# Sums of a stick-breaking attention: fp32 matmuls in four-byte passes, or a rounded high and low part

## What is computed

```python
z = jnp.einsum('bqhd,bkhd->bhqk', q_blk, kh).astype(jnp.float32) * scale
mask = k_pos[None, :] < q_pos[:, None]
log_keep = jnp.where(mask, jax.nn.log_sigmoid(-z), 0.0)
between = lax.cumsum(log_keep, axis=3, reverse=True) - log_keep
a = jnp.where(mask, jnp.exp(jax.nn.log_sigmoid(z) + between), 0.0)
return jnp.einsum('bhqk,bhkd->bqhd', a.astype(vh.dtype), vh)
```

## Time and profile before

| | us |
|---|---|
| Time before, median of 3 runs | 1922.7 (1922.46 to 1922.76) |
| The profiled execution, its own time | 1923.37 |
| Span of its profile | 1921.6 |
| TensorE busy | 1907.6 (99%) |
| VectorE busy | 1290.8 (67%) |
| ScalarE busy | 1030.5 (54%) |
| GpSimd busy | 188.0 (10%) |
| First stick layer, from the logits of pair 0 to the wait at the end of `second` | 1192 to 1242 |
| Second stick layer, the same | 1660 to 1710 |

### The profile page before, as it was taken

One profiled execution on the slowest core, in us unless ns is written; L12 is line 12 of the kernel. 1 busy time (PEld: TensorE's weight loads), 2 busy tenths in 40 slices (PEclk: granted clock), 3 DMA queues, 4 the chain that ended last, 5 costly groups with the idle time before them and its releaser, 6 DMA issues.

```text
span 1921.6 us, 27900 instructions
## 1 busy us (share of the span) xinstructions
PE 1907.6 (99%) x10702; PEld 1657.5 (86%) x10702; DVE 1290.8 (67%) x1348; ACT 1030.5 (54%) x1193; POOL 188.0 (10%) x163
## 2 busy tenths in 40 slices
PE   9999999999999999999999999999999999999998
PEld 8888889888888887788888889888888888988887
DVE  5866766766776677666676666776667666667665
ACT  5544564544554457654464446754455445665443
POOL 2800122100010001100010001210001000301000
PEclk9999999999999999999999999999999999999999
DMA  8655644555565553555556566366555556645653
GB/s 307 221 188 184 195 154 149 198 179 196 190 204 190 185 162 122 180 192 196 197 181 205 184 193 201 114 208 199 182 194 197 181 190 198 197 132 186 193 183 105
DMA packets 262420, 356.19 MB, mean 185 GB/s; under 512 B 9040, under 2 KB 230736, under 8 KB 262352
## 3 DMA queue, kind: packets, MB, share of 16 engines
q1 hardware_dynamic: 258752, 342.15, 54.6%
q0 software_dynamic: 3600, 13.11, 1.9%
HBM read 354.18 MB, written 1.05 MB: 185 GB/s over the span
## 4 chain that ended last, share of the span: by engine, by line
PE 87%; DVE 1%; ACT 1%; issue 0%; DVEq 0%; POOLq 0%; POOL 0%
PE down L585 26%; PE gate_banks L464 13%; PE up_banks L464 12%; PE gate_banks L469 7%; PE up_banks L469 6%; PE up_banks L527 4%; PE up_banks L448 3%; PE up_banks L449 3%; PE up_banks L450 3%; PE up_banks L533 2%; PE gate_banks L625 1%; PE gate_banks L655 1%; PE up_banks L479 0%; PE up_banks L481 0%; PE up_banks L480 0%
## 5 line engine op out<-in xcount | busy, mean ns | idle before, releaser
L1445 DVE TENSOR_TENSOR w_lo<-raw,w_hi 128x2048 fp32r<-128x2048 f32 x309 | 706.7, 2290 | 285.8 <-ACT w_hi L1028 285.7
L1028 ACT ACTIVATE w_hi<-raw 128x2048 fp32r<-128x2048 f32 x321 | 611.4, 1905 | 211.6 <-PE down L585 176.9
L464 PE MATMUL gate_banks<-h_both,w_hi 128*128 128x512 f32 x1280 | 305.9, 391 | 0.0
L464 PEld LDWEIGHTS gate_banks<-h_both,w_hi 128*128 128x128 f32 x1280 | 235.7, 188 | 46.1
L464 PE MATMUL up_banks<-h_both,w_hi 128*128 128x512 f32 x1152 | 273.7, 390 | 0.0
L585 PE MATMUL down<-w_hi,m_hi 128*128 128x512 f32 x832 | 269.2, 395 | 2.2 <-DVE m_lo L1538 1.0
L585 PE MATMUL down<-w_lo,m_hi 128*128 128x512 f32 x832 | 265.4, 390 | 0.0
L585 PE MATMUL down<-w_hi,m_lo 128*128 128x512 f32 x832 | 265.2, 390 | 0.0
L464 PEld LDWEIGHTS up_banks<-h_both,w_hi 128*128 128x128 f32 x1152 | 215.7, 188 | 44.5
L585 PEld LDWEIGHTS down<-w_hi,m_lo 128*128 128x128 f32 x832 | 156.2, 188 | 33.3
L585 PEld LDWEIGHTS down<-w_lo,m_hi 128*128 128x128 f32 x832 | 156.3, 188 | 33.0
(11 more groups left out here) (245 smaller groups left out, 2155.5 us busy)
## 6 DMA issues: line engine op xcount, KB each, us to landing
raw<-in_ffn_w_gu SPq DMA_DIRECT2D x88, 1024.0 KB, 5.1
raw<-in_ffn_w_down SPq DMA_DIRECT2D x88, 1024.0 KB, 4.9
raw<-in_ffn_w_gate SPq DMA_DIRECT2D x44, 1024.0 KB, 5.3
raw<-in_ffn_w_up SPq DMA_DIRECT2D x44, 1024.0 KB, 5.3
raw<-in_w_in SPq DMA_DIRECT2D x20, 1024.0 KB, 5.4
raw<-in_ret_w_in SPq DMA_DIRECT2D x13, 1024.0 KB, 5.4
raw<-in_w_o SPq DMA_DIRECT2D x8, 1024.0 KB, 5.0
raw<-in_w_out SPq DMA_DIRECT2D x8, 1024.0 KB, 4.9
```

The costliest lines, as they stand in the source:

```text
L464: mm(banks[:, j * 2 * S:(j + 1) * 2 * S], w_hi[:, r, c:c + P], h_both[:, k, :, :].rearrange("p a b -> p (a b)"), start=(k == 0), stop=(k = ...
L1028: act_fn(w_hi[:, r, 0:width], raw[:, r, 0:width], ACT.Copy).then_inc(hi_ready, 1)
L1445: v.tensor_tensor(w_lo[:, r, 0:width], raw[:, r, 0:width], w_hi[:, r, 0:width].bitcast(f32), ALU.subtract).then_inc(lo_ready, 1)
```

## The change

The sums of a pair are no longer done in plain fp32. ScalarE copies `z_lk` to a high part in fp32r (`keep_high`), VectorE subtracts it to get a low part (`keep_low`), and TensorE multiplies both with the triangle (384 columns in one matmul) and with the ones (128 columns), with weights that are an fp32r copy of the two constants (`exact`, made once in each layer). The parts lie in the then unused rows 4 to 7 of `m_hi` and `m_lo`. At the end of the layer `pair_min(3)` stands ahead of `convolve(0)`, and the low part of the pool ahead of `convolve(1)`.

```diff
+        lk_hi = m_hi[:, 4:7, :].rearrange("p a b -> p (a b)").rearrange("p (a b) -> p a b", a=2)
+        lk_lo = m_lo[:, 4:7, :].rearrange("p a b -> p (a b)").rearrange("p (a b) -> p a b", a=2)
+        exact = m_hi[:, 7, :]
...
                     def pair_sums(s):
-                        pe.wait_ge(s_lk, c0 + s + 1)
-                        tri, ones = cst("tri"), cst("ones")
-                        for g in range(2):
-                            lk, z = z_lk[:, g, :], mid[2 * (s % 2) + g]
-                            mm(z[:, 0:S], tri, lk[:, 0:S], start=False, stop=True, skip_group_check=True)
-                            mm(z[:, P:S], ones, lk[:, S:CAUSAL], start=False, stop=True, skip_group_check=True)
-                            last = mm(z[:, S:CAUSAL], tri, lk[:, S:CAUSAL], start=False, stop=True, skip_group_check=True)
+                        for ready, lk in ((s_lk_hi, lk_hi), (s_lk_lo, lk_lo)):
+                            for g in range(2):
+                                pe.wait_ge(ready, 2 * (c0 + s) + g + 1)
+                                mm(mid[2 * (s % 2) + g][:, 0:CAUSAL], exact[:, 0:P], lk[:, g, :], start=False, stop=True, skip_group_check=True)
+                            for g in range(2):
+                                last = mm(mid[2 * (s % 2) + g][:, P:S], exact[:, P:2 * P], lk[:, g, S:CAUSAL], start=False, stop=True, skip_group_check=True)
                         last.then_inc(s_cs, 1)
...
+                        def keep_high(s):
+                            for g in range(2):
+                                sc.wait_ge(s_lk, 2 * (c0 + s) + g + 1)
+                                act_fn(lk_hi[:, g, :], z_lk[:, g, :], ACT.Copy).then_inc(s_lk_hi, 1)
                         pair_log(0)
                         high(b + 7)
+                        keep_high(0)
                         high(b + 8)
                         pair_exp(0)
                         pair_log(1)
                         pair_high(0)
+                        keep_high(1)
                         high(b + 9)
                         pair_exp(1)
                         pair_log(2)
                         high(b + 10)
                         pair_high(1)
+                        keep_high(2)
                         high(b + 11)
                         pair_exp(2)
                         pair_log(3)
                         pair_high(2)
+                        keep_high(3)
                         high(b + 12)
...
+                        ve.wait_ge(const_in, 16)
+                        for i, name in enumerate(("tri", "ones")):
+                            v.tensor_copy(exact[:, i * P:(i + 1) * P], cst(name)).then_inc(exact_ready, 1)
                         slot_out(2)
...
+                        def keep_low(s):
+                            for g in range(2):
+                                ve.wait_ge(s_lk_hi, 2 * (c0 + s) + g + 1)
+                                v.tensor_tensor(lk_lo[:, g, :], z_lk[:, g, :], lk_hi[:, g, :].bitcast(f32), ALU.subtract).then_inc(s_lk_lo, 1)
                         pair_keep(0)
+                        keep_low(0)
                         slot_out(4)
                         low(b + 7)
                         slot_out(5)
                         pair_min(0)
                         low(b + 8)
                         pair_keep(1)
+                        keep_low(1)
                         slot_out(6)
...
+                        pair_min(3)
                         convolve(0)
-                        pair_min(3)
-                        convolve(1)
                         ve.wait_ge(pool_hi, 2 * (sticks + 1))
                         for j in range(2):
                             v.scalar_tensor_tensor(m_lo[:, 6 + j, :], bank0[:, j * S:(j + 1) * S], small[:, j, 3:4],
                                                    m_hi[:, 6 + j, :].bitcast(f32), ALU.mult, ALU.subtract).then_inc(pool_lo, 1)
+                        convolve(1)
                         low(b + 12)
```

More of the change, by code:

```diff
@@ L258, in build @@
         s_z, s_abs, s_ln, s_lk = sem("s_z"), sem("s_abs"), sem("s_ln"), sem("s_lk")
+        s_lk_hi, s_lk_lo = sem("s_lk_hi"), sem("s_lk_lo")
+        exact_ready = sem("exact_ready")
         s_cs, s_min, s_exp, s_out, s_hi, s_lo = (sem(n) for n in ("s_cs", "s_min", "s_exp", "s_out", "s_hi", "s_lo"))
@@ L886, in pair_sums @@
                     def pair_sums(s):
-                        pe.wait_ge(s_lk, c0 + s + 1)
-                        if c0 + s == 0:
-                            pe.wait_ge(const_in, 16)
-                        tri, ones = cst("tri"), cst("ones")
-                        for g in range(2):
-                            lk, z = z_lk[:, g, :], mid[2 * (s % 2) + g]
-                            mm(z[:, 0:S], tri, lk[:, 0:S], start=False, stop=True, skip_group_check=True)
-                            mm(z[:, P:S], ones, lk[:, S:CAUSAL], start=False, stop=True, skip_group_check=True)
-                            last = mm(z[:, S:CAUSAL], tri, lk[:, S:CAUSAL], start=False, stop=True, skip_group_check=True)
+                        if s == 0:
+                            pe.wait_ge(exact_ready, 2 * sticks + 2)
+                        for ready, lk in ((s_lk_hi, lk_hi), (s_lk_lo, lk_lo)):
[4 more added lines that the diff above has]
+                                last = mm(mid[2 * (s % 2) + g][:, P:S], exact[:, P:2 * P], lk[:, g, S:CAUSAL], start=False, stop=True, skip_group_check=True)
                         last.then_inc(s_cs, 1)
@@ L1399, in pair_log @@
                             sc.wait_ge(s_abs, 3 * (c0 + s) + 2)
-                            wait(sc, s_lk, c0 + s)
+                            wait(sc, s_lk, 2 * (c0 + s))
                             act_fn(z_ln, z_abs, ACT.Ln, bias=1.0).then_inc(s_abs, 1)
+                        def keep_high(s):
+                            for g in range(2):
+                                sc.wait_ge(s_lk, 2 * (c0 + s) + g + 1)
+                                act_fn(lk_hi[:, g, :], z_lk[:, g, :], ACT.Copy).then_inc(s_lk_hi, 1)
                         pair_log(0)
                         high(b + 7)
+                        keep_high(0)
                         high(b + 8)
@@ L1910, in pair_keep @@
                             for g in range(2):
-                                last = v.tensor_tensor(z_lk[:, g, :], z_ln[:, g, :], cst("negmask"), ALU.mult)
-                            last.then_inc(s_lk, 1)
+                                v.tensor_tensor(z_lk[:, g, :], z_ln[:, g, :], cst("negmask"), ALU.mult).then_inc(s_lk, 1)
+                        def keep_low(s):
+                            for g in range(2):
+                                ve.wait_ge(s_lk_hi, 2 * (c0 + s) + g + 1)
+                                v.tensor_tensor(lk_lo[:, g, :], z_lk[:, g, :], lk_hi[:, g, :].bitcast(f32), ALU.subtract).then_inc(s_lk_lo, 1)
                         pair_keep(0)
+                        keep_low(0)
                         slot_out(4)
@@ L1925, in _ @@
                         pair_keep(2)
+                        keep_low(2)
                         slot_out(7)
@@ L1932, in _ @@
                         pair_keep(3)
+                        keep_low(3)
                         slot_out(9)
```

## The result

| | before | after |
|---|---|---|
| Time, median of 18 runs (us) | 1922.59 (1922.33 to 1923.18) | 1926.46 (1925.20 to 1927.34) |
| Span of the profiled execution | 1921.6 | 1924.6 |

The ratio is 1.0019, with a 95% interval of 1.0013 to 1.0026. The change costs 3.9 us where 1.8 were forecast. The interval leaves 1 out, so the loss is real; it is just as large as the 3.8 us that the prediction took as the least that can be told from no change.

A forecast was written before the change was run, and what follows sets the result against it. TensorE, busy 99% of the span, was taken as the bound. Each of two layers ends 0.9 us late: +1.8 on 1923.4 gives 1925.2, and 1924.5 on the median, 0.7 lower; range 1919.7 to 1926.7.

The forecast's parts named there:

- a rival given 8%, the clock: Behind pair 1, TensorE's idling drops the clock to 1.2 GHz for 4 us: 2 us a layer, 1928.5; 8%.
- What TensorE saves: Sums of each pair in 1.15 us against 1.75: a saving of 0.6 (bounds 0.2 and 0.8), 2.4 a layer.
- The Trainium skill's weight load of 107 ns: In the sums, a rule pricing each 128-column matmul at 0.107 us; 0.11 was taken, from transposes.
- Pair 0: First pair of a layer: no TensorE wait at the sums, but slot_out(4) and GpSimd's pool sums 1.2 us late.
- Pair 1: Second pair: keep_low meets GpSimd at the port, slot_out(6) ends at 1217.75, logits of pair 2 start 1.8 us late.
- The turns at the port: In pair 1, VectorE and GpSimd alternate by exclusive lock: L2070 takes 1.3 us, then keep_low, then L2071 1.28, then keep_low.
- The end of the layer: At pair 3, TensorE waits for pair_min(3) and goes on at 1242.85 instead of 1241.96, 0.9 us late.
- the longest-wait argument: For pair 1: a 2.0 us wait left the clock at 1.00, the longest stretch here is 1.5; falling clock given 8%.
- The price given to it: Behind pair 1, 4 us at 1.2 GHz do what would have taken 2: a cost of 2 us a layer.
- The reorder at the end: Layer's end: with convolve(0) ahead of pair_min(3), TensorE would go on 1.8 us later still; the move costs nothing.
- The rival of little loss at the port: In pair 1, VectorE wins or lengthens by only 0.26 per instruction; TensorE goes on 1.2 early, 1920.3 us; 25%.

The follow-up runs named there:

- run 3: Changed kernel with seven unused matmuls of 512 columns added between the high and the low sums of pair 1: 1924.05 us.
- run 4: Changed kernel with the old order at the end of the layer, convolve(0) ahead of pair_min(3) and the pool's low part behind convolve(1): 1930.31 us.
- runs 4 and 8: The second of these: changed kernel with slot_out(4) moved ahead of keep_low(0) on VectorE, 1924.62 us. The first is run 4.
- run 5: Changed kernel with high and low parts still made but unused, TensorE summing in plain fp32 as before the change: 1925.99 us.
- runs 6 and 7: Changed kernel with low(b+8) moved behind pair_min(1): 1922.60 us; the same with pair_min(3) also ahead of the product conv_u: 1920.99 us.
- run 9: Changed kernel with slot_out(4) moved ahead of pair_keep(0), where VectorE stands idle: 1920.88 us.

## Why the prediction was right, and where it fell short

The mechanism that the prediction named is the one that the runs show, and its steps in a layer hold to 0.3 us. That the time fell into the range is in part luck: it lies above the forecast's own range (1923.5 to 1925.3), because a rival given 8%, the clock, came on top of the forecast at a smaller price than it was given.

- **What TensorE saves**: 0.6 per pair forecast, 0.65 measured. The 128-column matmuls of fp32r cost less than the 0.11 taken: two L900 take 0.17 us, 0.085 each, and two L898 0.36, as forecast.
- **The Trainium skill's weight load of 107 ns** (TensorE: Matmul & The Clock Gate, section LDWEIGHTS) was taken in the prediction as the price of each 128-column matmul. The trace has another price for these matmuls, 0.085 us as the mean of two that follow a long one; the measurement decides. It made 0.02 us per matmul.
- **Pair 0**: `slot_out(4)` 1.2 late by the forecast. It starts at 1200.69, and with the layer's 0.77 that is 1.16 late; GpSimd's sums moved with it. No wait in pair 0, as forecast.
- **Pair 1**: the logits of pair 2 1.8 late by the forecast, 1.57 measured, by the very instructions that were named. The turns at the port went as forecast: GpSimd, once waiting, is let in between two instructions of VectorE. `slot_out(6)` ends at 1216.76, with the 0.77 at 1217.5, forecast 1217.75. The rule of the Trainium skill (SBUF — State Buffer, section Who interferes with whom) agrees: L1934 with two SBUF operands is blocked, L1925 with one is not.
- **The end of the layer**: the forecast was 0.9 late. With the clock held (run 3) TensorE goes on at 1241.72 and the layer starts at 1192.31, 49.41 us, 0.6 late. The changed kernel has 1.9, and the difference is the clock's.
- **The step that fell short** is the longest-wait argument: "The longest wait in the trace, 2.0 us, left the granted clock at 1.00, and here the longest single stretch is 1.5", which made the clock a rival of 8%. The idle time itself came as forecast: 2.6 of 3.8 us by the distances (forecast 3.1 of 4.2), the longest stretch 1.36 (forecast 1.5); the view of waits has 0.23, 0.38 and 1.10. And yet the clock fell in both layers. One wait that had left the clock up, near the start of the program, said nothing about this place: in run 4 the clock stayed up behind a wait of 2.31 us and fell behind one of 2.12. The price given to it, 2 us a layer for 4 us at the lower level, was too high: 3.4 us at the lower level, 1.2 us a layer by run 3. Forecast without the clock 1924.5, measured without it 1924.05; with it 1926.46.
- **The reorder at the end**: said to be worth 1.8 a layer, measured 1.9 by the medians and 1.7 by the trace where the clock stayed up.
- **The rival of little loss at the port** would have had 1920.3; the changed kernel without the pool's sums has 1919.2.

What stays open: when exactly the clock falls. The changed kernel's 18 executions spread over 2.1 us and the filled one's 11 over 1.1. The profiles of runs 4 and 8 show it fall in one of two layers that have the same waits, so it depends on something besides these waits, which no run here isolates.

## What to carry to other kernels

A step that shifts two engines by different amounts can move a harmless overlap onto the critical path: lay the timelines of VectorE and GpSimd beside each other and look at which instructions with two SBUF operands will meet, not only at how many there are. When a faster operation brings nothing, time it once with the suspected neighbour left out, in both kernels; here that turned a loss of 3.9 us into a gain of 3.5 and pointed to the remedy, the place of one instruction, which gave 5.6 us back, and of a second, which gave 1.7. And when TensorE will idle, do not trust that the clock stays because one longer wait elsewhere left it up: fill the idle time with unused matmuls in one run, and the difference is the clock's price.

## What the runs showed of the hardware

- The granted clock fell to 1.2 GHz for 3.4 us after three waits of 0.23, 0.38 and 1.10 us in both layers of the changed kernel's profile. After the same waits in run 4 it stayed at 1.00 in one layer and fell for 6.8 us in the other. It stayed at 1.00 in both layers with one wait of 1.48 us (run 5) and with one of 1.1 (runs 6 and 7), and behind one of 2.31 (run 4, first layer); behind one of 2.12 (run 4, second layer) it fell.
- At the start of the program the view gives a clock of 1.00, and yet the matmuls of 512 columns (L723) lie 0.43 us apart until 4.6 us, and 0.23 from then on. The wait of 2.0 us on which the prediction leaned begins 3 us later, and behind it they lie 0.23 apart again: the clock was up, but the first rows of that column are not proof of it.
- Matmuls whose results nobody reads made the kernel 2.4 us faster (run 3).
- An fp32r matmul of 128 columns costs 0.085 us in a row of two behind longer ones, one of 384 columns 0.18; plain fp32 0.22 for 128 (an eighth of 1.75).
- GpSimd and VectorE take turns at the port one instruction at a time: two subtractions of 0.5 us each took 3.18 beside two GpSimd instructions that show as 1.47 each. GpSimd is held up as well: its copy of two columns (L2092) takes 0.18 us in run 9, where VectorE stands idle, and 2.17 beside a `low` of 2.28.
